# Adding each pass's expert rows to a table of token sums in HBM, instead of storing them and gathering them at the end

## The reference, cut to what matters

```
top_vals, top_idx = lax.top_k(logits, 4);  gates = softmax(top_vals)
for every expert e and every token t that chose it:
    gt  = min(h[t] @ w_gate[e] + b_gate[e], 7)
    up  = clip(h[t] @ w_up[e] + b_up[e], -7, 7)
    hid = gt * sigmoid(1.702 * gt) * (up + 1)
    ffn[t] += gate[t, e] * (hid @ w_down[e] + b_down[e])
out = layer_norm(2 ** 0.25 * h + ffn) * ln2_g + ln2_b
```

## Time and profile before

| | |
|---|---|
| median of 3 runs | 2426.29 us (2425.88 to 2428.72) |
| the profiled execution's own time | 2425.69 us |
| its span in the profile | 2423.9 us |
| PE / DVE / ACT / POOL busy | 93% / 33% / 27% / 8% of the span |
| stage_experts | from 1328.15 us to the end |

### The profile page before, as it was taken

One profiled execution on the slowest core, in us unless ns is written; L12 is line 12 of the kernel. 1 busy time (PEld: TensorE's weight loads), 2 busy tenths in 40 slices (PEclk: granted clock), 3 DMA queues, 4 the chain that ended last, 5 costly groups with the idle time before them and its releaser, 6 DMA issues. The chain is left out here.

```text
span 2423.9 us, 27490 instructions
## 1 busy us (share of the span) xinstructions
PE 2261.3 (93%) x9835; PEld 1082.9 (45%) x9836; DVE 810.9 (33%) x1548; ACT 652.4 (27%) x854; POOL 204.1 (8%) x239
## 2 busy tenths in 40 slices
PE   6998999989899999989896999999999999999991
PEld 4444656634567576535455333333333333333330
DVE  1411556644443454532434212112112111111215
ACT  1211222220100000001301344344343444344440
POOL 1003111100000000000300100000000000000003
PEclk8999999979899999999996999999999999999996
DMA  8344333220631321141006869999999999999995
GB/s 333 138 188 110 79 88 105 74 74 0 244 116 70 123 86 70 52 158 38 0 27 248 345 240 394 420 423 406 422 423 408 423 406 424 422 407 423 422 402 189
DMA packets 139862, 570.75 MB, mean 235 GB/s; under 512 B 12279, under 2 KB 47276, under 8 KB 88588
## 3 DMA queue, kind: packets, MB, share of 16 engines
q1 hardware_dynamic: 123584, 527.89, 55.1%
q0 software_dynamic: 6432, 21.66, 2.5%
q10 hardware_dynamic: 9772, 20.25, 2.2%
HBM read 545.57 MB, written 24.18 MB: 235 GB/s over the span
## 5 line engine op out<-in xcount | busy, mean ns | idle before, releaser
L2411 ACT COPY expert_ring<-expert_ring 128x2048 f32 x180 | 331.7, 1896 | 75.0 <-DMA expert_ring<-in_w_gate_dram 63.3
L2479 PE MATMUL banks<-expert_ring,slot_xT_gate 128*64 128x512 f32 x1440 | 328.4, 598 | 1.6 <-issue 0.9
L2479 PE MATMUL banks<-expert_ring,slot_xT_up 128*64 128x512 f32 x1440 | 320.0, 596 | 3.3 <-DMA expert_ring<-in_w_up_dram 3.3
L2479 PE MATMUL banks<-expert_ring,hiddenT 128*64 128x512 f32 x1440 | 316.7, 592 | 2.1 <-DVE hiddenT L2554 2.1
L2479 PEld LDWEIGHTS banks<-expert_ring,hiddenT 128*64 128x64 f32 x1440 | 103.3, 137 | 207.3 <-issue 205.0
L2479 PEld LDWEIGHTS banks<-expert_ring,slot_xT_up 128*64 128x64 f32 x1440 | 98.9, 137 | 192.5 <-issue 182.0
L2479 PEld LDWEIGHTS banks<-expert_ring,slot_xT_gate 128*64 128x64 f32 x1440 | 100.1, 137 | 188.7 <-issue 181.3
L2562 DVE TENSOR_SCALAR slot_y<-banks,slot_gates 128x512 f32<-128x512 f32 x45 | 33.8, 751 | 410.2 <-PE banks L2479 410.2
L486 PE MATMUL banks<-hT,weight_ring 128*128 128x512 f32 x320 | 142.6, 606 | 2.3 <-PEq L2649 2.3
L2547 DVE TENSOR_TENSOR up_act_T<-banks,expert_bias_T 128x512 f32<-128x512 f32 x45 | 31.1, 692 | 304.1 <-PE banks L2441 304.1
L1355 PE MATMUL banks<-hT,weight_ring 128*128 128x256 f32 x512 | 115.8, 387 | 4.2 <-PEq L2649 3.3
(11 more groups left out here) (440 smaller groups left out, 2474.3 us busy)
## 6 DMA issues: line engine op xcount, KB each, us to landing
expert_ring<-in_w_gate_dram SPq DMA_DIRECT2D x128, 1024.0 KB, 13.7
expert_ring<-in_w_up_dram SPq DMA_DIRECT2D x128, 1024.0 KB, 13.7
expert_ring<-in_w_down_dram SPq DMA_DIRECT2D x128, 1024.0 KB, 11.0
weight_ring<-in_w_ada_dram SPq DMA_DIRECT2D x12, 2048.0 KB, 11.2
weight_ring<-in_w_in_dram SPq DMA_DIRECT2D x8, 2048.0 KB, 14.8
weight_ring<-in_w_ff_in_dram SPq DMA_DIRECT2D x8, 2048.0 KB, 11.2
weight_ring<-in_w_ff_out_dram SPq DMA_DIRECT2D x8, 2048.0 KB, 13.1
weight_ring<-in_w_in_dram SPq DMA_DIRECT2D x24, 512.0 KB, 6.6
```

The costliest lines, as they stand in the source:

```text
L2411: nc.scalar.copy(flat_ring[:, c * size:(c + 1) * size], flat_ring[:, bass.ds(source + c * size, size)])\
L2479: x = nc.tensor.matmul(ps[h * CAP:(h + 1) * CAP, bank, :], lhs[:, k % 4, (k // 4) * CAP:(k // 4 + 1) * CAP], X.ring[:, m, k, h * HALF:(h + ...
```

## The change

`y_dram` goes. In its place stands `sum_dram`, a table of 1024 token half rows, laid out as `h_dram`, and after them as many spare rows. The spare half is zeroed in the FFN stage (4 DMAs of 512 KB where 16 stood). `slot_rows` replaces `choice_row`: the table row of each row of a slot, or a spare row of its own where the slot is not full. It takes five small DVE instructions at the end of `stage_route`, and two go.

In `stage_experts` ACT writes the four tiles `ALPHA * h + bias` to the table in the first two passes (`to_table`, 512 KB each), and PE and DVE make the bias sums a little earlier. ACT's `store` goes. Instead POOL issues `add_rows(i-2)` in `body(i)`, behind `gather(i + 1)`: an indirect DMA that adds the 128 half rows of `slot_y` into the table. In body 1, which has nothing to add yet, POOL waits there for all four table tiles. After the loop come the last two adds; then SP loads the four tiles of the table into `G.X`, and DVE goes straight to the layer norm.

```diff
@@ ffn stage, ACT (SP waits for spare_zeroed, 16 * T, in place of y_zeroed)
-            for r in range(EXPERTS * CAP, MAX_SLOTS * CAP, P):
-                n = min(P, MAX_SLOTS * CAP - r)
-                act.dma_start(G.y_dram[r:r + n, :], zeros[0:n, :]).then_inc(G.y_zeroed, 16)
+            for t in range(T, 2 * T):
+                rows = G.sum_dram[2 * t * P:2 * (t + 1) * P, :].rearrange("(p h) n -> p (h n)", h=2)
+                act.dma_start(rows, zeros[:]).then_inc(G.spare_zeroed, 16)
@@ stage_route, DVE
-            step(nc.vector.scalar_tensor_tensor(out=rowf[:], in0=sl[:], scalar=float(CAP), in1=col[:], op0=ALU.mult,
-                                                op1=ALU.add))
-            nc.vector.tensor_copy(G.choice_row[:], rowf[:])
...
             nc.vector.tensor_scalar(G.slot_tokens[:], ps[:, 3, 0:LIST], upper[:, 0:1], None, ALU.add).then_inc(list_ok, 1)
+            nc.vector.tensor_scalar(token_row[:], ps[:, 3, 0:LIST], upper[:, 0:1], None, ALU.add)
+            step(nc.vector.tensor_scalar(empty[:], ps[:, 3, LIST:2 * LIST], 0.0, None, ALU.is_equal))
+            step(nc.vector.tensor_scalar(spare[:], token_row[:], -1.0, tok[:, 0:1], ALU.mult, ALU.add))
+            step(nc.vector.scalar_tensor_tensor(out=spare[:], in0=spare[:], scalar=2.0 * S, in1=empty[:], op0=ALU.add,
+                                                op1=ALU.mult))
+            nc.vector.tensor_tensor(G.slot_rows[:], token_row[:], spare[:], ALU.add)
@@ stage_experts, SP, after the weights and the two gains
+            sp.wait_ge(q["stored"], 1)
+            for t in range(T):
+                sp.dma_start(G.X[:, t, :], table(t)).then_inc(sums_in[t], 16)
@@ POOL
+            def add_rows(i):
+                at = slice(i, i + 1) if isinstance(i, int) else bass.ds(i, 1)
+                pool.wait_ge(q["y_ok"], i + 1)
+                nc.gpsimd.tensor_copy(rows[:], G.slot_rows[:, at]).then_inc(rows_ok, 1)
+                pool.wait_ge(rows_ok, i + 1)
+                pool.wait_ge(held_rows, i + 1)
+                nc.gpsimd.tensor_tensor(row_tick[:], tick[:, 0:1], tick[:, 0:1], ALU.add).then_inc(held_rows, 1)
+                nc.gpsimd.indirect_dma_start(G.sum_dram[:, :], bass.IndirectOffsetOnAxis(rows[:, 0:1], 0), y[:], None,
+                                             compute_op=ALU.add).then_inc(G.y_out, 16)
             def body(i, first):
                 pool.wait_ge(q["x_turned"], i + 1)
                 gather(i + 1)
+                if first:
+                    pool.wait_ge(table_in, 16 * T)
+                else:
+                    add_rows(i - 2)
...
-            pool.wait_ge(G.y_out, last * 32 + 32)
+            add_rows(last - 1)
+            add_rows(last)
+            pool.wait_ge(G.y_out, last * 16 + 16)
...
-            four(0)
-            choice(G.X[:, end, :], end, 0, sum_in, True)
...
@@ ACT
-            def store(i):
...
+            def to_table(t):
+                act.wait_ge(q["bias_added"], t + 1)
+                act.dma_start(table(t), G.X[:, t, :]).then_inc(table_in, 16)
...
                 move_gate(i + 1)
-                if not (isinstance(i, int) and i == 0):
-                    store(i - 1)
                 sigmoid(i)
+                if first:
+                    to_table(2 * i)
                 up_copy(i)
+                if first:
+                    to_table(2 * i + 1)
                 x_for_up(i + 1)
@@ PE
                 turn_x(i + 1)
+                if first and not zero:
+                    bias_sum(2)
                 product(xTg, B_G, 0, range(PARTS // 2, PARTS), now, None if zero else i)
+                if first:
+                    bias_sum(0 if zero else 3)
                 if not zero:
                     down(i - 1, before, not first)
-                if first:
-                    bias_sum(0 if zero else 2)
...
-                if first:
-                    bias_sum(1 if zero else 3)
+                if zero:
+                    bias_sum(1)
@@ DVE: result(i) waits for y_out 16 * i (was 32 * i); add_bias(2) and (3) stand before result(0)
-                for k in range(TOP_K if t < T - 1 else 0):
-                    dve.wait_ge(row_in[t * TOP_K + k], 16)
-                    step(nc.vector.tensor_tensor(x, x, plain(t * TOP_K + k), ALU.add))
...
+                dve.wait_ge(sums_in[t], 16)
                 nc.vector.bn_stats(stats[:, t, 0, :], x[:, 0:HALF])
```

More of the change, by code:

```diff
@@ L1266, in _ @@
             G.W.upto(sp, G.W.index[("q2",)] + RING)
-            sp.wait_ge(G.y_zeroed, 16 * (-(-(MAX_SLOTS - EXPERTS) * CAP // P)))
+            sp.wait_ge(G.spare_zeroed, 16 * T)
         @block.gpsimd
@@ L1995, in stage_route @@
         col = sb("choice_col", [P, TK])
-        rowf = sb("choice_rowf", [P, TK])
+        token_row = sb("slot_token_row", [P, LIST])
+        spare = sb("slot_spare", [P, LIST])
+        empty = sb("slot_empty", [P, LIST])
         colhot = sb("col_onehot", [P, TK, P])
@@ L2248, in stage_experts, with table @@
         held = sem("ex_held")
[L2249 to L2254, removed]
+        rows, row_tick = sb("slot_rows_now", [P, 1], I32), sb("row_tick", [1, 1])
+        rows_ok, held_rows, table_in = sem("ex_rows_ok"), sem("ex_held_rows"), sem("ex_table_in")
+        sums_in = [sem(f"ex_sums_in{t}") for t in range(T)]
+        def table(t):
+            return G.sum_dram[2 * t * P:2 * (t + 1) * P, :].rearrange("(p h) n -> p (h n)", h=2)
         stats = sb("ln2b_stats", [P, T, 2, 6])
@@ L2321, in gather @@
                     .then_inc(G.xg_in, 16)
+            nc.gpsimd.memset(row_tick[:], 0.0).then_inc(held_rows, 1)
+            def add_rows(i):
[7 more added lines that the diff above has]
+                                             compute_op=ALU.add).then_inc(G.y_out, 16)
             def body(i, first):
@@ L2429, in _ @@
             last = loop(act, body)
-            store(last)
             nc.scalar.activation(tick[:, 3:4], tick[:, 0:1], ACT.Sqrt).then_inc(q["root_ok"], 1)
@@ L2559, in result @@
                 if not first:
-                    dve.wait_ge(G.y_out, i * 32)
+                    dve.wait_ge(G.y_out, i * 16)
                 at = slice(i, i + 1) if isinstance(i, int) else bass.ds(i, 1)
@@ L2571, in body @@
                 hidden(i - 1)
+                if first:
+                    add_bias(2)
+                    add_bias(3)
                 result(i - 1, first)
                 dve.wait_ge(q["hT_ok"], i)
-                if first:
-                    add_bias(2)
                 gate(i)
-                if first:
-                    add_bias(3)
             dve.wait_ge(G.h_out, 16 * T)
@@ L2628, in make_shared @@
     G.h_dram = nc.dram_tensor("h_halves", [2 * S, HALF], F32)
-    G.y_dram = nc.dram_tensor("expert_rows", [MAX_SLOTS * CAP, D], F32)
-    G.h_out, G.y_out, G.y_zeroed = sem("h_out"), sem("y_out"), sem("y_zeroed")
+    G.sum_dram = nc.dram_tensor("token_sums", [4 * S, HALF], F32)
+    G.h_out, G.y_out, G.spare_zeroed = sem("h_out"), sem("y_out"), sem("spare_zeroed")
     G.sums_out, G.decays_ok, G.dtf_in = sem("sums_out"), sem("decays_ok"), sem("dtf_in")
@@ L2698, in build @@
         G.gates = sbc(ctx, "choice_gates", [P, T, TOP_K])
-        G.choice_row = sbc(ctx, "choice_row", [P, T * TOP_K], I32)
+        G.slot_rows = sbc(ctx, "slot_rows", [P, LIST], I32)
         G.slot_tokens = sbc(ctx, "slot_tokens", [P, LIST], I32)
```

## The result

The changed kernel takes 2441.1 us (2438.5 to 2443.9, 4 runs), the kernel before 2427.5 us (4 runs) on the same chip: ratio 1.0052, 95% interval 1.0039 to 1.0065. It is 0.5% slower. The profiled execution took 2439.1 us, its span is 2437.3 against 2423.9. The forecast was 2429.0 with a range up to 2440.

A forecast was written before the change was run, and what follows sets the result against it. It took PE and DMA both to be at their limit in the loop, DMA making each period 2 us longer than PE's work. End -20.7, loop +10 and start +14 gave +3.3: 2429.0 us profiled, range 2418 to 2440.

The forecast's parts named there:

- The start: Body 1: POOL's wait for the table tiles delays gather(3), halting PE 12.6 us; with slower products after it, +14 us.
- slow restart: After the halt at the start, PE's first 16 products take 5.08 us against 3.65, 1.4 us more.
- DMA was idle for part of these windows: At the start DMA has room but cannot give the lost time back; the ring is full and loads wait for PE.
- The end: From the last result to the span's end: 29.6 us for 50.3, a gain of 20.7 us.
- The rule of the Trainium skill: Last add's landing: 2.0 us plus bytes at 436 GB/s, 2.6 us; the prediction took 4.6 instead.
- The small edits: Route stage instructions, fewer zero stores in the FFN stage and moved bias sums: costed at nothing.
- The loop: Expert loop: adds lengthen each period of seven passes by 2.0 us, over five waits +10 us.
- The 2.2 us of air take up part: Loop: of 4.2 us extra per period, adds before a bandwidth dip (2.1 us) fit into it, leaving 2.0.
- The prices: Loop: an add costs double by the byte, 0.6 us more than a store per pass, 4.2 us a period.
- the dips stay: Slower rival: dips come from SP's in-order waits, so adds pay in full, 21 us for 10, 2440; chance 0.2.
- The kind of wait: Sign in the loop: PE's five waits for up weights grow by 2 us each, with dips gone.
- the second read: Loop: an add's extra DMA time beyond a store, for reading the old rows; taken as 0.6 us a pass.

The follow-up runs named there:

- kernel 1: The changed kernel with POOL's wait for the table tiles moved from body 1 to body 2, behind gather(3); 2427.0 us, 0.9990 of the kernel before.
- kernel 2: The changed kernel with each pass's adding scatter made a plain indirect write, so the sums are missing; 2419.5 us, 0.9957 of the kernel before.
- 10: kernel 1 with the single gate load issued ahead of the up load, GATE_TURN (0, 0, 2, 0, 2); 2426.9 us, 0.9992 of the kernel before.
- 13: kernel 1 with a second adding indirect DMA of the same rows per pass, to a scratch table; 2476.0 us, 1.0178 of the kernel before.
- 14: kernel 1 with a second, plain scatter of the same rows per pass, to a scratch table; 2449.8 us, 1.0070 of the kernel before.
- kernel 3: The kernel before, with POOL also writing slot_y (256 KB) to a scratch tensor each pass by plain DMA; 2447.3 us, 1.0072 of the kernel before.
- 8: The kernel before with its order of loads changed to GATE_TURN (1, 1, 2, 1, 2); 2454.2 us, 1.0095 of the kernel before.
- 11: The kernel before with the copies of the up product and of up's turned rows moved from ACT to DVE; 2431.1 us, 1.0007.
- kernel 9: kernel 1 with the copies of the up product and of up's turned rows moved from ACT to DVE; 2428.7 us, 0.9997 of the kernel before.
- 5 to 8: Runs of eight gate loads parted by up loads: three orders on kernel 1 (2438.9, 2448.2, 2445.3 us), one on the kernel before (2454.2 us).
- 12: kernel 9 with the single gate load issued ahead of the up load, GATE_TURN (0, 0, 2, 0, 2); 2429.0 us, 0.9996 of the kernel before.

## Why the prediction failed, point by point

Its sum for the profiled execution was 2429.0 and 2439.1 came: 10.1 us more.

**The start was right, and so were its steps.** A halt of 11.5 us for the 12.6 forecast, plus a slow restart of 5.92 us for 3.65, 2.3 for 1.4; that the two misses nearly cancel is luck. The first product behind it, of `down`, begins at 1406.71, 15.4 us later than before; 0.9 of it was there at `turn_x(1)`. That leaves 14.5 for 14, and kernel 1 gives the same 14.5 by moving one wait. That DMA was idle for part of these windows did not help, as the prediction had it.

**The end was right:** 30.0 us for 29.6. The lone add landed in 4.80 for 4.6, the first tile in 3.63 for 3.4, each layer norm took 4.2 to 4.3. The rule of the Trainium skill that stood beside it (DMA: Bandwidth & Descriptors, Anatomy of one DMA, SWDGE path) gives an estimate of 2.6 us; kernel 2's last plain scatter, at 2.7 us, agrees with it, while the add does not.

**The small edits** were costed at nothing. The 0.9 us at `turn_x(1)` are no evidence against that: kernels 1 and 10, alike up to there, reach it 4.5 us apart.

**The loop is the step that failed:** "The 2.2 us of air take up part", and the rest of that sentence, by which the adds ahead of a dip fit into it. The prices were right: double by the byte, 0.6 us more a pass, 4.2 a period (0.62 and 4.4 by kernels 13 and 14). But the period grew by 4.0, not by 2.0, so the air took up some 0.4 us. From the end of the halt at the start (1391.33 before, 1406.71 after, the starts of the same product) to the last result (2373.58 and 2407.28), 982.3 us became 1000.6, 18.3 more. By groups of seven passes from the third `result` on, the changed kernel falls behind by 0.6, 5.1, 3.5, 4.3, 4.0 and 0.7 us, which is all of it within the rounding.

1.7 of the 18.3 is the last `down` product, and it is not the change's. Before (first row) and after (second) it stands behind the same wait of 2.1 us for DVE, and took 7.09 and 8.78 us:

```profile
2365.50:2372.59 7.09, 7.08 (x32) 2.20 (x32) 0.00 (x0) 0.00 (x0) 0.00 (x0) 1.00 0.01 3
2397.50:2406.28 8.78, 8.78 (x32) 2.61 (x32) 0.00 (x0) 0.00 (x0) 0.00 (x0) 0.81 0.03 14
```

The granted clock (the third number from the end) differs. Of the 16 traces of this document ten have the long form, 8.60 to 9.13 us, among them kernels 2, 3, 8 and 11, which add nothing, and six the short one, kernels 1 and 9 with all their adds among them. So it does not hang on the adds, and the runs show no cause that would tell the two forms apart. The 16.6 us that are left stand where the prediction has 10. The end saved 0.4 less than forecast, and the sum of the misses is 0.5 + 0.9 + 6.6 + 1.7 + 0.4 = 10.1.

This is near the rival *the dips stay*, at a chance of 0.2: 21 for 10 and 2440. The loop cost less than its 21, 16.6 us; that the time still meets its 2440 owes something to the 1.7 and the 0.9 above, which is luck. Its mechanism can be read in the trace. SP's issues and ACT's moves in the changed kernel's timeline at the dip of 1950 to 1956 us:

```profile
1944.14 8.46 SPq L2209 DMA_DIRECT2D expert_ring<-in_w_gate_dram  x4
1945.25 1.90 ACT L2413 COPY expert_ring<-expert_ring 128x2048 f32 x1 [1.28 <-DMA expert_ring<-in_w_gate_dram]
...
1950.21 1.90 ACT L2413 COPY expert_ring<-expert_ring 128x2048 f32 x1 [0.57 <-DMA expert_ring<-in_w_gate_dram]
...
1952.79 2.02 SPq L2209 DMA_DIRECT2D expert_ring<-in_w_up_dram  x4
```

Its bandwidth from 1936 to 1960 us, in slices of 0.6:

```profile
GB/s 410 423 423 437 423 437 437 437 423 423 396 416 430 423 437 410 437 410 396 437 423 396 382 410 410 355 369 369 300 369 256 328 246 348 410 406 423 410 437 437
```

SP may issue a gate part only when the part before it, in the same place, has landed and been moved, and behind these four stand the four up loads. For 8.5 us it adds a load only as fast as ACT moves one, and the queue runs down; at 1952.79 it can go on. A dip made by such an order is no store of free time: a queue that is longer lands the gate parts later, ACT moves them later, and the dip moves along with them. That is read from the trace and not shown by a run that removes the dips: the orders without the eight in a row (5 to 8) put another wait of SP in the place of this one, and none was faster.

In the kernel before, SP stands at the same wait, but what lies behind it is another thing:

```profile
1984.04 0.58 ACT L2385 COPY gate_product<-banks 128x512 f32<-128x512 f32 x1 [7.01 <-PE banks L2479]
1985.45 7.33 ACT L2411 COPY expert_ring<-expert_ring 128x2048 f32 x4 [0.34 <-issue]
1987.52 5.75 SPq L2204 DMA_DIRECT2D expert_ring<-in_w_gate_dram  x4
```

All four gate parts had landed, and ACT came to them only when PE had finished the gate product. The rate falls to 60 GB/s in a slice of 0.55 us near 1988. So this dip was set by PE's schedule, just as the prediction has it, and adds ahead of it could have fitted in. With the adds the parts land later, ACT waits for them (1.28 and 0.57 us above), and between 1880 and 2050 us there are two dips, near 1953 and 2018, for one. The step took the cause of the dips for fixed; by these two traces it changed under the load.

An estimate by bytes gives the same size. A period needs 60 loads of 1 MB and 14 transfers of 256 KB, each add counted twice: at 423 GB/s, the rate of the full slices, 157.4 us before and 161.7 in the changed kernel. The periods are longer than that by 2.2 and 1.9 us. In kernel 3 it is 1.9 again, and in kernels 13 and 14 it is 2.5, so their prices of 1.36 and 0.74 us hold some 0.1 us of deeper dips. Why 0.3 to 0.4 us of the air is taken up and no more stays open.

The prediction weighed this rival too low for a reason that one can see in it: it read the dips as spare capacity since they are the only places where the rate falls, and did not look at which instruction of SP stood there. The rows with SP's issues at a dip would have said that SP stood at a wait there, though not that its cause would change.

**The kind of wait** also came otherwise: not up weights grown by 2 us each, but the up copy behind the gate's moves. It was not what cost the time (9, 10, 12).

**Is there a gain to be had?** Kernel 1 at 0.9990 (0.9981 to 0.9998) of the kernel before is faster than the change by 0.6% and ahead of the kernel before by 0.1%, less than the 0.2% that the prediction takes as what can be told. The end gives 20 us back and the second read takes most of it in the loop; kernel 2, without the additions, is 10 us faster than the kernel before, and the halt at the start is still in it.

## What to carry to other kernels

- An accumulating DMA is to be counted as about two transfers (here 1.36 us for 0.74 in the loop, 4.8 for 2.7 alone); a tail that it saves is paid for in a loop that has no DMA time to give. Multiply by the passes first.
- Before you count a dip in the bandwidth as room for more transfers, look at what the issuing queue waits for there, and whether that wait will still be the same one under the new load. Here the dips of 2.2 us a period took up no more than 0.4 us.
- When a loop is bound by transfers, the wait that PE shows can be only the place where the lateness surfaces. Here taking that wait away moved it; the period tells whether anything was won.

## What the runs showed of the hardware

- An add of 256 KB to HBM costs a loop bound by transfers 1.36 us, a plain scatter of the same 0.74. Under load they land in 9.3 and 7.2 us (medians), alone at the end in 4.8 and 2.7. POOL is busy issuing it for 1.84 us (median), 1.25 without the addition.
- PE comes back slowly also after short halts, which the prediction had only for a long one. After 4.25 us without work 16 products took 4.33 us for 3.65, and the two groups of four turns ahead of them 1.1 us each for 0.66; after 11.5 us they took 5.92. After waits of 2.1 to 2.3 us the last product was slow in ten traces of sixteen. The windows of the changed kernel show it in PEclk, the granted clock as a share of 2.4 GHz: 1.00 is that level, and one below it says that part of the stretch was at 1.2.

```profile
1912.70:1917.00 4.30, 4.30 (x19) 1.47 (x20) 1.22 (x3) 0.00 (x0) 2.00 (x3) 0.83 1.01 429
1920.00:1940.00 20.00, 20.00 (x100) 7.22 (x98) 4.37 (x7) 7.86 (x8) 4.27 (x6) 1.00 1.02 409
1400.00:1407.00 7.00, 7.00 (x22) 2.54 (x24) 0.00 (x0) 0.07 (x1) 1.40 (x3) 0.60 0.11 41
```

  In this loop, bound by transfers, it cost nothing: kernel 9 has none of the halts of 4 us and the same period.
